# An encoder step on one core: the weight remainder computed in two halves, and five pieces of work put in another order

## What is computed

```python
def layer(h, p_i, hist, S0, offset, g_mix, w_in, w_pool, pool_scale, g_gn, w_out, g_ple, w_pg, w_ple):
    hn = rmsnorm(h, g_mix)
    z = hn @ w_in
    u, gp, q, k, v, gr = jnp.split(z, 6, axis=-1)
    y_pool, new_hist = pool_mix(u, hist, offset, w_pool, pool_scale)
    y_pool = y_pool * jax.nn.silu(gp.astype(jnp.float32))
    ...
    o, S_new = retention(qr, kr, v.reshape(B, L, RET_HEADS, RET_DV), S0)
    ...                                  # group norm of o, times silu(gr)
    mix = jnp.concatenate([y_pool, o], axis=-1).astype(h.dtype)
    h = h + mix @ w_out
    gate = jax.nn.sigmoid((rmsnorm(h, g_ple) @ w_pg).astype(jnp.float32))
    h = h + (gate * (p_i @ w_ple).astype(jnp.float32)).astype(h.dtype)
    return h, new_hist, S_new
```

## Time and profile before

| | |
|---|---|
| median of 3 executions | 2465.92 us (2464.02 to 2466.3) |
| the profiled execution | 2466.18 us, its span 2464.4 us |
| mean granted TensorE clock | 0.997 of full speed |
| TensorE busy | 2444.0 us, 99% |
| VectorE busy | 1035.4 us, 42% |
| ScalarE busy | 642.3 us, 26% |
| GpSimd busy | 217.9 us, 9% |

### The profile page before, as it was taken

How to read it: one execution, slowest core, us unless ns; L and a number is a source line. 1 busy time by engine, 2 the same in 40 slices (tenths; PEclk the granted TensorE clock), 3 DMA queues, 4 the chain that set the end, 5 groups by cost and what they waited for, 6 DMA issues and landing times.

```text
span 2464.4 us, 27265 instructions
## 1 busy us (share of the span) xinstructions
PE 2444.0 (99%) x11188; PEld 2011.3 (82%) x11188; DVE 1035.4 (42%) x1584; ACT 642.3 (26%) x1005; POOL 217.9 (9%) x329
## 2 busy tenths in 40 slices
PE   9999999999999999999999999999999999999997
PEld 7888888888888888888888888888888788888886
DVE  6343343443455234444543433433434542344444
ACT  6212212211233113322322112112122232242223
POOL 2101101101101000000010110110110100000001
PEclk9999999999999999999999999999999999999998
DMA  7343343243243333223242432433432433322322
GB/s 229 100 121 118 85 124 118 80 129 118 80 126 117 99 102 103 83 75 111 82 150 77 134 107 86 134 107 86 134 107 83 133 121 111 107 69 86 94 69 103
DMA packets 180396, 264.84 MB, mean 107 GB/s; under 512 B 16720, under 2 KB 128656, under 8 KB 178992
## 3 DMA queue, kind: packets, MB, share of 16 engines
q1 hardware_dynamic: 143040, 171.87, 23.2%
q0 software_dynamic: 23376, 77.79, 9.9%
q10 hardware_dynamic: 13856, 13.44, 2.3%
HBM read 226.02 MB, written 37.02 MB: 107 GB/s over the span
## 4 chain that ended last, share of the span: by engine, by line
PE 97%; DVE 2%; issue 0%; DMA 0%; ACT 0%; DVEq 0%; ACTq 0%
PE acc L1365 88%; PE side L1365 8%; PE osb L1599 1%; PE side L1449 0%; PE side L1562 0%; PE side L1502 0%; DVE st L1073 0%; DVE Sp L1089 0%; DVE Ss L1097 0%; DMA Z<-in_x_t 0%; DVE HT L1337 0%; PE osb L1365 0%; DVE HT L1241 0%; DVE mv L1079 0%; DVE Z L1252 0%
## 5 line engine op out<-in xcount | busy, mean ns | idle before, releaser
L1365 PE MATMUL acc<-Ahi,Whi 128*128 128x512 f32 x2048 | 811.4, 396 | 3.6 <-DVE Wlo L848 1.9
L1365 PE MATMUL acc<-Alo,Whi 128*128 128x512 f32 x2048 | 798.9, 390 | 0.0
L1365 PE MATMUL acc<-Ahi,Wlo 128*128 128x512 f32 x2048 | 798.3, 390 | 0.0
L487 ACT ACTIVATE Whi<-raw 128x1024 fp32r<-128x1024 f32 x319 | 338.4, 1061 | 1484.1 <-PE acc L1365 1478.9
L848 DVE TENSOR_TENSOR Wlo<-raw,Whi 128x1024 fp32r<-128x1024 f32 x319 | 391.0, 1226 | 740.3 <-ACT Whi L487 740.0
L1365 PEld LDWEIGHTS acc<-Ahi,Whi 128*128 128x128 f32 x2048 | 385.1, 188 | 87.9 <-issue 6.3
L1365 PE MATMUL acc<-Whi,Ahi 128*128 128x512 f32 x1152 | 451.4, 392 | 0.0
L1365 PEld LDWEIGHTS acc<-Alo,Whi 128*128 128x128 f32 x2048 | 384.7, 188 | 81.3
L1365 PEld LDWEIGHTS acc<-Ahi,Wlo 128*128 128x128 f32 x2048 | 385.3, 188 | 79.4 <-issue 1.0
L1365 PE MATMUL acc<-Whi,Alo 128*128 128x512 f32 x1152 | 448.7, 389 | 0.0
L1365 PE MATMUL acc<-Wlo,Ahi 128*128 128x512 f32 x1152 | 448.2, 389 | 0.0
(11 more groups left out here) (196 smaller groups left out, 1434.6 us busy)
## 6 DMA issues: line engine op xcount, KB each, us to landing
raw<-in_w_in SPq DMA_DIRECT2D x384, 256.0 KB, 3.0
raw<-in_w_out SPq DMA_DIRECT2D x128, 256.0 KB, 3.3
raw<-in_w_pg SPq DMA_DIRECT2D x128, 256.0 KB, 3.2
Ss<-in_state_ret POOLq DMA_DIRECT2D x64, 256.0 KB, 5.1
out_new_ret_sample<-Ss POOLq DMA_DIRECT2D x64, 256.0 KB, 3.0
kv_parts<-stage ACTq DMA_DIRECT2D x16, 256.0 KB, 2.5
Z<-in_x_t POOLq DMA_DIRECT2D x4, 1024.0 KB, 5.5
Ss<-in_w_ple POOLq DMA_DIRECT2D x8, 512.0 KB, 5.2
```

Of the source, the lines that this page charges most:

```text
L487: nc.scalar.activation(Whi[:, p % 2], raw[:, p % 2], ACT.Copy).then_inc(w_hi, 1)
L1365: return nc.tensor.matmul(out, lhsT, rhs, start=start, stop=stop)
```

## The change

1. **Halves.** `lo(m)` becomes `lo(m, kk)`: one instruction of 512 columns for one k-tile. The first half of a pair stands at the even step ahead of `jobs(s)`, the second at the odd step, that is behind the even step's jobs and ahead of the odd step's. `w_lo` counts halves. TensorE waits for both before a pair's first matmul, where it goes by pairs, and for one at a time where it goes step by step. SyncE's load waits for both halves.
2. **First tile.** ScalarE converts the first weights ahead of the first prompt tile, the sample part of the first tile has a semaphore of its own (`xs_first`), SyncE and GpSimd wait for the prompt part alone, TensorE's first matmul waits for the two high parts, its second for the weight's remainder and its third for the tile's remainder. 16 warm-up matmuls instead of 18.
3. **Block 5 of the states** is updated right after the last update of Sp, ahead of the sample output's statistics.
4. **Conversion 9** of the mixed output moves from step 13 of the last head's gate stream to step 0 of the first output stream, on ScalarE and VectorE.
5. **The last square** on ScalarE stands behind the second output tile, and VectorE's mean one output row later.

```diff
@@ sync
-                        sp.wait_ge(x_in[0], 32)
+                        sp.wait_ge(x_in[0], 16)
...
-                sp.wait_ge(w_lo, m + 1)
+                sp.wait_ge(w_lo, 2 * m)
@@ scalar
-            ac.wait_ge(x_in[0], 32)
-            nc.scalar.activation(Ahi[:, 0, 0:NP], HT[:, 0], ACT.Copy, scale=par[:, PC[0]:PC[0] + 1]).then_inc(a_hi, 1)
             ac.wait_ge(w_first, 16)
             ac.wait_ge(w_used, 1)
             nc.scalar.activation(Whi[:, 0, 0], raw[:, 0, 0], ACT.Copy).then_inc(first_hi, 1)
+            ac.wait_ge(x_in[0], 16)
+            nc.scalar.activation(Ahi[:, 0, 0:NP], HT[:, 0], ACT.Copy, scale=par[:, PC[0]:PC[0] + 1]).then_inc(a_hi, 1)
+            ac.wait_ge(xs_first, 16)
...
-                    if 10 <= s < 14:
+                    if 10 <= s < 13:
                         conv_hi(3 * l + 1, s - 4)
...
-                    for i in {1: (10,), 2: (11,), 3: (12,), 5: (13,), 7: (14,), 8: (15,)}.get(s, ()):
+                    for i in {0: (9,), 1: (10,), 2: (11,), 3: (12,), 5: (13,), 7: (14,), 8: (15,)}.get(s, ()):
@@ vector
-            def lo(m):
+            def lo(m, kk):
+
                 if m == DEPTH * G_LAYER * PAIRS:
                     return
-                p = m % PAIRS
-                ve.wait_ge(w_hi, m + 1)
-                nc.vector.tensor_tensor(Wlo[:, p % 2], raw[:, p % 2], Whi[:, p % 2].bitcast(F32), ALU.subtract) \
+                p = m % 2
+                if kk == 0:
+                    ve.wait_ge(w_hi, m + 1)
+                nc.vector.tensor_tensor(Wlo[:, p, kk], raw[:, p, kk], Whi[:, p, kk].bitcast(F32), ALU.subtract) \
                     .then_inc(w_lo, 1)
...
-                    if s % 2 == 0:
-                        lo(q * PAIRS + s // 2 + 1)
+                    lo(q * PAIRS + s // 2 + 1, s % 2)
                     jobs(s)
...
                             update(3)
+                            update_stream(5)
                             ve.wait_ge(os_ready, hh + 1)
...
-                        for b in {12: (4,), 13: (5,), 14: (6, 7)}.get(s, ()):
+                        for b in {12: (4,), 14: (6, 7)}.get(s, ()):
@@ tensor
-            for _ in range(18):
+            for _ in range(16):
...
+                def weights(s):
+                    pe.wait_ge(w_lo, q * KT + s + 3)
...
                 for s in range(0 if q else 4, KT - 2, 2):
 
-                    pe.wait_ge(w_lo, q * PAIRS + (s // 2 + 3))
+                    weights(s + 1)
                     for t in range(NT):
```

More of the change, by code:

```diff
@@ L331, in _ @@
             po.memset(qTm[:], 0.0).then_inc(zeroed, 1)
-            po.wait_ge(x_in[0], 32)
+            po.wait_ge(x_in[0], 16)
             load_x(po, 2)
@@ L816, in _ @@
                                      scale=rstd[:, t:t + 1]).then_inc(yt_done, 1)
+                if i == 1:
+                    ac.wait_ge(h_new, H_NEW * DEPTH)
+                    nc.scalar.activation(vd[:].rearrange("p a b -> p (a b)"), HS[:, D - NW:D], ACT.Square,
+                                         accum_out=ssq[:, 3:4]).then_inc(ssq_done, 1)
             ac.wait_ge(gmul_done, 2)
@@ L823, in _ @@
         def _(ve):
-            ve.sem_inc(w_lo, 2)
+            ve.sem_inc(w_lo, 3)
             ve.sem_inc(side_free, 2)
@@ L933, in scaled @@
                 nc.vector.tensor_tensor(out, acc[:, t], rstd_row[:], ALU.mult).then_inc(acc_out["V"], 1)
-            ve.wait_ge(a_hi, 1)
-            residue(Alo[:, 0, 0:NP], HT[:, 0], 0, PC[0], Ahi[:, 0, 0:NP])
             ve.wait_ge(first_hi, 1)
@@ L939, in _ @@
                 .then_inc(first_lo, 1)
+            ve.wait_ge(a_hi, 1)
+            residue(Alo[:, 0, 0:NP], HT[:, 0], 0, PC[0], Ahi[:, 0, 0:NP]).then_inc(first_lo, 1)
             ve.wait_ge(first_hi, 2)
@@ L1339, in _ @@
                     .then_inc(y_done, 1)
-                if k == KTOK + 1:
+                if k == KTOK + 2:
                     ve.wait_ge(ssq_done, 2 * DEPTH * G_OUT + G_OUT)
@@ L1378, in tile @@
                         if t == 0:
-                            pe.wait_ge(first_lo, 1)
+                            pe.wait_ge(first_hi, 1)
+                            pe.wait_ge(a_hi, 1)
                         if t == NPT:
@@ L1390, in tile @@
                         mm(acc[:, t], hi[:, cols], Ahi[:, k, 0:NP], first, False)
+                        if q + s + t == 0:
+                            pe.wait_ge(first_lo, 1)
                         mm(acc[:, t], lo[:, cols], Ahi[:, k, 0:NP], False, False)
+                        if q + s + t == 0:
+                            pe.wait_ge(first_lo, 2)
                         done = mm(acc[:, t], hi[:, cols], Alo[:, k, 0:NP], False, last)
@@ L1409, in stream @@
                         jobs(s)
-                    pe.wait_ge(w_lo, q * PAIRS + PAIRS + 2)
+                    weights(KT - 1)
                     for t in range(NT):
@@ L1416, in stream @@
                     for s in range(4):
-                        if s == 1 or s == 2:
-                            pe.wait_ge(w_lo, s // 2 + 3)
+                        if s:
+                            weights(s)
                         for t in range(NT):
```

9 lines of the change are left out of this document (3 added, 6 removed).

## The result

The changed kernel takes 2467.98 us, the median of 20 executions (2466.6 to 2471.2), against 2465.61 us for the kernel before (20 executions, 2463.83 to 2466.33). The medians lie 2.4 us apart. The ratio by the comparison over all executions is 1.0013, interval 1.0007 to 1.0019, that is slower by 1.7 to 4.7 us; by the 0.2% that the prediction asked for, this is "same". The prediction said 2467.8. The profiled execution took 2466.6, its span is 2464.8.

What follows compares the result with a forecast made beforehand. TensorE, busy 2444.0 of 2464.4 us, was taken to bound the kernel. Terms -1.3 -1.7 +3.0 +1.7 +0.1 +0.1 sum to +1.9 us: 2468.1 on the profiled run, stated as 2467.8 from the median; range 2463.8 to 2471.5.

Steps and rivals of the forecast that it cites:

- (a): Second pair of each kv stream, eight times: second half ends late behind the query rotation, TensorE waits and restarts; +3.0 us.
- (b): Second pair of layer 1's first stream: second half stands behind a residue and four small ones; +1.7 us.
- (c): The end, last pair: the two halves follow each other with nothing between; +0.1 us.
- bank update: Gate streams, six heads: earlier block 5 update saves 0.38 us each, partly given back; net -1.3 us, bounds 0 and -2.3.
- boundary: Last head of each layer: moved conversion lets the next stream's first matmul start 0.85 us earlier, twice; -1.7 us.
- start: Kernel's start: TensorE's 0.74 us gain all given back at third and next pairs; +0.1 us, bounds -0.9 and +1.2.
- tail: Output end: first two transfers start 1.3 us earlier, but full DMA engines end as before; 0, bounds -0.7 and +0.3.
- The clock did not fall in (b): Rival: layer 1's first stream's 1.6 us stop lowers the granted clock, costing 1.6 us more; 2469.4 us, chance 0.2.
- The gains are kept whole: Rival: bank updates and start gain more, kv streams' second pairs lose less; 2465.0 us, chance 0.22.
- The slower case: Rival: late input landing stops the third pair 2.3 us, clock falls there and in layer 1's first stream; 2472.1, chance 0.1.
- The faster case: Rival: neither (a) nor (b) bites and the clock holds after the end's stop; 2459.7 us, chance 0.04.

Runs made afterwards that it cites:

- the halves at once: Changed kernel with both halves issued together ahead of the jobs in step 0 of the kv streams and layer 1's first stream: 2463.66 us.
- split wait: Changed kernel with the moved wait, TensorE also waiting for each pair's second half only after the first token tile of its first k-tile: 2460.41 us.
- the moved wait: TensorE waits for the last pair's remainder only ahead of that pair's matmuls: kernel before with this 2462.96 us, changed kernel with this 2465.38.
- the halves alone: Kernel before with only the remainder cut into halves (part 1 of the change), nothing else moved: 2472.3 us, ratio 1.003.

## Why the prediction held

The time came out 0.2 us from the number given, and that is closer than its steps were.

| step | predicted | profiled execution | what the runs add |
|---|---|---|---|
| (a) second pair of each kv stream | +3.0 | 0.44 + 7 x 0.38 = +3.1 | gone with the halves at once, and with TensorE's split wait |
| (b) layer 1's first stream | +1.7 | +1.7 | the same |
| (c) the end | +0.1 | +0.1 | |
| bank update, six heads | -1.3 | 6 x (-0.38 + 0.14) = -1.4 | hangs on the halves: 6 x (-0.38 + 0.34) without them |
| boundary, two heads | -1.7 | 2 x (-0.89 + 0.08) = -1.6 | -0.35 and -0.7 without the halves |
| start | +0.1 | -0.1 | +0.3 and +0.6 in two other traces of the same start; +0.4 to +0.8 by what is left |
| tail | 0 | -0.3 | 0 |
| steps under 0.06 us | none | +0.6 | +0.6 in the pair with the moved wait; 0.4 less where the kv stops are gone |

**(a), (b) and (c)** held to a tenth, and so did their cause: the place of the second half behind the jobs, with a wait on TensorE that asks for both halves. The price was read from rows of before alone: the end of the last job, the 0.69 of a half, TensorE's next start, and the 0.11 of restart. That last small term is 0.9 us of the 3.1.

**The bank update and the boundary** held in size, and the bank update with the reason given, that the first half is short and so GpSimd's power moves up by 0.54 (at 191.00, with TensorE 0.39 later than in the earlier trace rows ahead of the gain). VectorE gained more by it than the 0.13 of the sum, 0.24. At the boundary the moved conversion, priced at 0.66, did less by itself in layer 0, and the halves did part of it: in the halves alone each boundary's stop is 0.2 shorter. I then forgot the halves' share in the expectations of two runs: with the remainder whole VectorE is 0.04 earlier in the six heads and not 0.24, and -3.2 and -4.4 were each too much by about 2.

**The start** was the mis-sized term: +0.1 within bounds of -0.9 and +1.2. Its mechanism (an early TensorE runs into the third pair's second half) is what the trace shows, 21.78 against a forecast of 21.95, although TensorE got there 1.2 us ahead and not the 0.74 of the sum. But one execution is one landing of the input. Three traces have this same start: against before's trace they stand at -0.1 (the changed kernel), +0.3 (with the moved wait) and +0.6 us (with the halves at once) by 30 us. The measured terms but the start and the tail sum to +2.5 with the small steps; the clusters say +3.25 and the pair of runs with the moved wait +2.9, so some +0.4 to +0.8 is left for the start, the upper part of the range. That it is the start and not another place is argued from these three traces, between which little else differs beyond what was edited; it is not shown for the median execution.

**The small steps** had no term. 0.11 was the first interval behind a stop; several of the next ones are longer by 0.01 each. Behind the eight kv stops that makes 0.42 us, and in the traces where TensorE doesn't stop there (the halves at once, the split wait) it is 0.0. So a kv stop costs 0.16 beyond its wait and not 0.11. The remaining 0.2 lies around the six heads and the two boundaries.

**Why then 0.2 from the number?** The medians lie 2.4 apart, less than the 3.25 between clusters, because more of the changed kernel's executions kept their clock (12 of 20) than of before's (9 of 20). With 20 executions of before its median is also 0.3 lower than the 2465.92 of three that I added to. The true difference without the clock is 3 us and not 1.9; that the number came out to 0.2 us is partly luck: the missing 0.6 of small steps and the start's share were offset by the clock's chances and by a base that was 0.3 high.

**The rivals.** The clock did not fall in (b) in any trace. In one execution out of 20, the slowest (2471.2), it may have fallen somewhere a second time: its mean clock is 0.996, an estimate of two falls of 0.0007 from the 0.9976 of the profiled execution; no trace of it was kept. "The gains are kept whole" is out, (a) is not smaller. The slower case had its place right, the start, and too large a price: no stop there reached 1.9 us in a trace. The faster case is out too: (a) and (b) both bit. Its time doesn't follow from the terms either: the forecast without (a) and (b) and with the clock kept is 2467.8 - 4.7 - 1.6 = 2461.5, not 2459.7.

**The rule on exposed latency** (the Trainium skill, "VectorE: DVE Perf Modes", section on the TRN2 errata) would have made each half cost its whole 0.69. In the changed kernel two halves in a row have one record of 1.28 at the end (two times 0.69 would be 1.38), so the next starts 0.60 after; the measurement decides. In (a) the last row of the rotation moves from 256.89 to 256.54 while TensorE stands 0.18 later, 0.53 in all, as the 0.60 has it; with 0.69 it would be 0.45.

## What to carry to other kernels

Cutting one instruction into two pays where its reader waits for the parts one at a time, or where a small job that another engine waits for stood behind the whole (the variance in the gate streams, 0.2 us a head). Here one and the same VectorE program was 2.4 us slower (2465.38) or 2.6 us faster (2460.41) than the old one (2462.96) by where TensorE's wait stood; parts 2 to 5, worth 1.8 with the whole remainder, are in both. When the second part goes behind other work, list the places where that work is long and the reader close, and price each with the restart. And look at the one long stop in the list of waits first: moving a single wait past 6 matmuls gave 1.4 us, and by the times, which form one cluster, it kept the clock up there in every execution.

## What the hardware did that I had not expected

Seven of the traces have the stop of 1.9 to 2.0 us at the last pair. In six of them it was followed by a granted clock of 0.50 for some 3 us, in the seventh, the changed kernel's, it stayed at 1.00. The other seven, with the stop of 0.6 or less, all stay at 1.00. By the clusters about half of the executions of before are of either kind, some 1.6 us apart; no trace of an execution of before in its lower cluster was kept. The list's waits of 1.44 in layer 1's first stream and of 1.2 to 1.5 at the start left the clock alone in every trace. Of two profiled executions 1.5 us of difference can so be a matter of chance, more than most of the terms that were to be read from them.
